# The merge stage of a one-core decoder layer: two passes over the column tiles, branch products from high and low parts, and the first weight tiles fetched during the attention

## The reference, cut to what matters

```
h = rms_norm(x, ln_mix_pre); z = h @ w_in
o_nsa = attend(...)                       # 512 features
o_gm  = u * chunk_spatial_mix(v, ...)     # 512 features
g_a, g_b = split(sigmoid(merge columns of z), 2)     # 2 x 1024 features
mixed = (g_a * (o_nsa @ w_branch_nsa) + g_b * (o_gm @ w_branch_gm)) @ w_out
x = x + rms_norm(mixed, ln_mix_post)
```

## Time and profile before

| what | us |
|---|---|
| runs of the kernel before: median (lowest to highest, 3 runs) | 2273.68 (2272.06 to 2279.49) |
| the profiled execution: its own time | 2271.01 |
| the profiled execution: span from first to last instruction | 2269.2 |
| merge stage: first matmul to last branch matmul's end | 884.61 to 1179.1 |
| merge stage, one tile in steady state | 18.29 |
| mean granted TensorE clock over the span | 0.953 |

### The profile page before, as it was taken

One profiled execution on the slowest core, in us unless ns is written; L12 is line 12 of the kernel. 1 busy time (PEld: TensorE's weight loads), 2 busy tenths in 40 slices (PEclk: granted clock), 3 DMA queues, 4 the chain that ended last, 5 costly groups with the idle time before them and its releaser, 6 DMA issues. The chain is left out here.

```text
span 2269.2 us, 33313 instructions
## 1 busy us (share of the span) xinstructions
PE 2082.9 (92%) x13581; PEld 1937.6 (85%) x13581; DVE 746.0 (33%) x1439; ACT 503.9 (22%) x917; POOL 571.6 (25%) x471
## 2 busy tenths in 40 slices
PE   6999999985688887999999799999999999997897
PEld 5999989953566776888879799999999999997786
DVE  3202533333766764111132343202321321234412
ACT  4112011122466564101021231110000000011323
POOL 1222400000344443112213213333323333331120
PEclk6999999987799998999999799999999999998898
DMA  5323264124200001111113121111111111113011
GB/s 165 113 75 125 53 217 161 62 110 166 82 1 2 2 1 29 48 44 42 42 46 111 49 94 46 37 56 47 44 42 54 47 35 58 47 35 126 24 46 77
DMA packets 164786, 150.88 MB, mean 66 GB/s; under 512 B 24747, under 2 KB 157389, under 8 KB 161934
## 3 DMA queue, kind: packets, MB, share of 16 engines
q1 hardware_dynamic: 160846, 111.68, 16.2%
q0 software_dynamic: 2304, 33.56, 3.7%
q10 hardware_dynamic: 1536, 4.23, 0.5%
HBM read 132.54 MB, written 21.10 MB: 68 GB/s over the span
## 5 line engine op out<-in xcount | busy, mean ns | idle before, releaser
L583 POOL CAST WS<-W 128x1024 fp32r<-128x1024 f32 (+2 forms) x126 | 124.7, 990 | 1139.8 <-PE ffn_acc L575 539.9
L575 PE MATMUL ffn_acc<-HH,WS 128*128 128x344 f32 x2112 | 394.8, 321 | 9.0 <-DVE HL L507 7.9
L575 PEld LDWEIGHTS ffn_acc<-HH,WS 128*128 128x128 f32 x2112 | 344.3, 189 | 9.4 <-issue 8.0
L585 POOL TENSOR_TENSOR WS<-W,WS 128x1024 fp32r<-128x1024 f32 (+2 forms) x126 | 297.2, 2358 | 10.1
L575 PE MATMUL ffn_acc<-HL,WS 128*128 128x344 f32 x1056 | 224.8, 321 | 0.0
L575 PE MATMUL ffn_acc<-AH,WS 128*128 128x344 f32 x1056 | 195.4, 320 | 0.0
L575 PE MATMUL proj_acc<-HH,WS 128*128 128x344 f32 x912 | 174.2, 323 | 6.2 <-DVE HL L507 6.2
L575 PEld LDWEIGHTS ffn_acc<-HL,WS 128*128 128x128 f32 x1056 | 179.4, 190 | 0.0
L575 PEld LDWEIGHTS ffn_acc<-AH,WS 128*128 128x128 f32 x1056 | 171.6, 188 | 0.0
L1844 POOL TENSOR_SCALAR Hr<-Hr,tiny,gtok 128x63 f32<-128x63 f32 (+4 forms) x192 | 124.4, 657 | 174.5 <-DVE tiny L1924 141.7
L575 PE MATMUL merge_acc<-HH,WS 128*128 128x344 f32 x768 | 149.6, 327 | 11.8 <-POOL WS L585 11.8
(11 more groups left out here) (374 smaller groups left out, 3163.6 us busy)
## 6 DMA issues: line engine op xcount, KB each, us to landing
W<-in_w_in SPq DMA_DIRECT2D x31, 512.0 KB, 4.1
W<-in_w_ffn_gate SPq DMA_DIRECT2D x22, 512.0 KB, 3.8
W<-in_w_ffn_up SPq DMA_DIRECT2D x22, 512.0 KB, 3.9
X<-kept_x SPq DMA_DIRECT2D x2, 4128.0 KB, 13.3
W<-in_w_ffn_down SPq DMA_DIRECT2D x16, 384.0 KB, 3.4
W<-in_w_ffn_down SPq DMA_DIRECT2D x16, 320.0 KB, 3.1
kept_x<-Z SPq DMA_DIRECT2D x1, 4128.0 KB, 15.6
Z<-kept_x SPq DMA_DIRECT2D x1, 4128.0 KB, 13.8
```

What stands on the lines that cost most here:

```text
L575: last = k.nc.tensor.matmul(acc[:, s, n, 0:NW], k.WS[:, ws, part, c, :], src[:, c, n * NW:(n + 1) * NW], start=(c == 0 and part == 0 and s ...
L583: k.nc.gpsimd.tensor_copy(k.WS[:, ws, 0, 0:nk, :], w).then_inc(hi_done, 1)
L585: k.nc.gpsimd.tensor_tensor(k.WS[:, ws, 1, 0:nk, :], w, k.WS[:, ws, 0, 0:nk, :].bitcast(F32), ALU.subtract).then_inc(split_done, 1)
```

## The change

The 16 tiles are no longer a loop; they are written out in the order j = 1 for m = 0 to 7, then j = 0 for m = 0 to 7. The first pass writes its gated product straight into `MT`, the second puts its own into `TM` and adds it to `MT`.

The branch product is made like the gate product. At the head of each pass ScalarE rounds the four chunks of the branch activation into `BH` (`high`), and VectorE subtracts them in place to get the low parts `OGL` or `ONL` (`lows`). GpSimd splits each branch weight tile into one buffer `WB`. TensorE issues the three products per chunk: 36 matmuls in place of 12. There is one `BH` for both passes: ScalarE makes the second pass's high parts behind the branch product of tile 7 (the eighth), and VectorE makes its low parts behind the scaling of tile 8 (the ninth).

SyncE fetches the gate weights and the branch weights of the first tile at the beginning of the attention into columns of the `kvtok` area that the attention leaves free. GpSimd splits the gate tile from there in two halves.

```diff
         k.WS = place("WS", "CW", [P, 2, 2, DC, P], F32R)
-        k.E = sb("E", [P, 5632])
+        k.E = place("E", "E", [P, 5632])
+        k.WB = place("WB", "E", [P, 2, 4, P], F32R, 4 * N)
+        k.BH = place("BH", "Z", [P, 4, N], F32R, 8 * N)
+        k.OGL = place("OGL", "Z", [P, 4, N], F32R, 13104)
+        k.ONL = place("ONL", "Z", [P, 4, N], F32R, 17232)
...
             sp.dma_start(k.X[:].rearrange("p c t -> p (c t)"), k.kept).then_inc(x_back, 16)
+            sp.dma_start(k.kvtok[:, 0:8, 256:384], weight(k.g["w_in"], GB0)).then_inc(k.first_in, 16)
+            sp.dma_start(k.kvtok[:, 0:4, 512:640], weight(k.g["w_branch_gm"], 0)).then_inc(k.first_in, 16)
+            sp.wait_ge(k.first_in, 32)
...
+        tiles = [(j, m) for j in (1, 0) for m in range(8)]
...
         @block.sync
         def _(sp):
+            for u, (j, m) in enumerate(tiles):
+                if u == 0:
+                    continue
+                if u > 1:
+                    sp.wait_ge(split_done, u)
+                sp.dma_start(k.W[:, 0, 0:8, :], weight(w, m * P + (GA0, GB0)[j])).then_inc(k.wfull[0], 16)
+                if u > 1:
+                    sp.wait_ge(bw_done, u)
...
         @block.tensor
         def _(pe):
+            for u, (j, m) in enumerate(tiles):
+                if u == 0:
+                    pe.wait_ge(split_half, 1)
+                    split_tile(k, acc, 0, 0, k.HH, k.HL, 4, more=True, wait=(pe, h.lo_done))
+                    pe.wait_ge(split_done, 1)
+                    split_tile(k, acc, 0, 0, k.HH, k.HL, DC, first=4, wait=(pe, h.lo_done)).then_inc(gates_done, 1)
+                else:
+                    pe.wait_ge(split_done, u + 1)
+
+                    pe.wait_ge(scaled, u)
+                    split_tile(k, acc, 0, u % 2, k.HH, k.HL, DC).then_inc(gates_done, 1)
+                pe.wait_ge(bw_done, u + 1)
+                if u:
+                    pe.wait_ge(gated, u)
+                for c in range(4):
+                    if m == 0:
+                        pe.wait_ge(b_lo, 4 * (1 - j) + c + 1)
+                    for part, src in ((0, k.BH), (0, low[j]), (1, k.BH)):
+                        for n in range(NT):
+                            last = nc.tensor.matmul(acc[:, 1, n, 0:NW], k.WB[:, part, c, :], src[:, c, n * NW:(n + 1) * NW],
...
         @block.gpsimd
         def _(pool):
+            pool.wait_ge(k.first_in, 32)
+            for b in range(2):
+                c = slice(4 * b, 4 * b + 4)
+                nc.gpsimd.tensor_copy(k.WS[:, 0, 0, c, :], first_gate[:, c, :]).then_inc(hi_done, 1)
...
+            for u, (j, m) in enumerate(tiles):
+                if u:
+                    pool.wait_ge(k.wfull[0], base[0] + 16 * u)
+                    if u >= 2:
+                        pool.wait_ge(gates_done, u - 1)
+                    split_weights(k, pool, 0, u % 2, DC, hi_done, u + 1, split_done)
...
+                    pool.wait_ge(k.wfull[1], base[1] + branch[0])
+                    pool.wait_ge(branch_done, u)
+                wb = k.W[:, 1, 0:4, :] if u else first_branch
+                nc.gpsimd.tensor_copy(k.WB[:, 0], wb).then_inc(bw_hi, 1)
+                pool.wait_ge(bw_hi, u + 1)
+                nc.gpsimd.tensor_tensor(k.WB[:, 1], wb, k.WB[:, 0].bitcast(F32), ALU.subtract).then_inc(bw_done, 1)
...
         @block.scalar
         def _(act):
...
+            high(1)
+            for u, (j, m) in enumerate(tiles):
+                if u == 8:
+                    act.wait_ge(branch_done, 8)
+                    high(0)
...
         @block.vector
         def _(dve):
...
+                nc.vector.tensor_tensor(tokens(SA[:, u % 2, :]), acc[:, 0, :, 0:NW], tokens(k.R1[:]), ALU.mult).then_inc(scaled, 1)
+                if u == 8:
+                    lows(0)
+                dve.wait_ge(sig, u + 1)
+                dve.wait_ge(branch_done, u + 1)
+                if j == 1:
+                    nc.vector.tensor_tensor(tokens(k.MT[:, m, :]), tokens(SA[:, u % 2, :]), acc[:, 1, :, 0:NW], ALU.mult).then_inc(gated, 1)
```

More of the change, by code:

```diff
@@ L104, in build @@
         base = -(-nc.sbuf_base // 32) * 32
-        sizes = {"X": DC * N, "H": DC * N, "Z": 21360, "W": 2048, "CW": 4096}
+        sizes = {"X": DC * N, "H": DC * N, "Z": 21360, "W": 2048, "CW": 4096, "E": 5632}
         sb("slab", [P, sum(sizes.values()) + 8])
@@ L126, in build @@
         k.WS = place("WS", "CW", [P, 2, 2, DC, P], F32R)
-        k.E = sb("E", [P, 5632])
+        k.E = place("E", "E", [P, 5632])
[3 more added lines that the diff above has]
+        k.ONL = place("ONL", "Z", [P, 4, N], F32R, 17232)
+        k.first_in = ctx.enter_context(nc.semaphore("first_in"))
         k.R1 = sb("R1", [P, N])
@@ L1959, in merge @@
         acc = st.psum("acc", [P, 2, NT, 512])
-        mm = st.sems("gates_done branch_done")
-        scaled, sig, gated, merged, slot_open, hi_done, split_done, slot_ok = st.sems(
-            "scaled sig gated merged slot_open hi_done split_done slot_ok")
+        gates_done, branch_done, scaled, sig, gated, merged, hi_done, split_half, split_done, bw_hi, bw_done, b_hi, b_lo = st.sems(
+            "gates_done branch_done scaled sig gated merged hi_done split_half split_done bw_hi bw_done b_hi b_lo")
         SA = chunks(k.E[:, 0:2 * N], 2)
@@ L1966, in merge @@
         base = list(k.wcount)
-        k.wcount[0] += 8 * 32 + 16
-        k.wcount[1] += 8 * 48
+        k.wcount[0] += 16 * 16
+        k.wcount[1] += 7 * 16 + 8 * 32
         nsa = g["w_branch_nsa"].rearrange("(gr c d) m -> gr d c m", gr=2, d=HD)
+        raw = (k.ON, k.OG)
+        low = (k.ONL, k.OGL)
+        tiles = [(j, m) for j in (1, 0) for m in range(8)]
+        first_gate, first_branch = k.kvtok[:, 0:8, 256:384], k.kvtok[:, 0:4, 512:640]
         block = st.block()
@@ L1973, in _ @@
         def _(sp):
[L1974 to L1987, removed]
+            for u, (j, m) in enumerate(tiles):
[6 more added lines that the diff above has]
+                    sp.wait_ge(bw_done, u)
+                if j == 0:
+                    for gr in range(2):
+                        sp.dma_start(k.W[gr * HD:(gr + 1) * HD, 1, 0:4, :], nsa[gr][:, :, m * P:(m + 1) * P]).then_inc(k.wfull[1], 16)
+                else:
+                    sp.dma_start(k.W[:, 1, 0:4, :], weight(g["w_branch_gm"], m * P)).then_inc(k.wfull[1], 16)
+            sp.wait_ge(split_done, 16)
             sp.dma_start(k.W[:, 0, 0:8, :], weight(g["w_out"], 0)).then_inc(k.wfull[0], 16)
@@ L1991, in _ @@
         def _(pe):
[L1992 to L2003, removed]
+            for u, (j, m) in enumerate(tiles):
[4 more added lines that the diff above has]
+                    split_tile(k, acc, 0, 0, k.HH, k.HL, DC, first=4, wait=(pe, h.lo_done)).then_inc(gates_done, 1)
+                else:
+                    pe.wait_ge(split_done, u + 1)
[10 more added lines that the diff above has]
+                            last = nc.tensor.matmul(acc[:, 1, n, 0:NW], k.WB[:, part, c, :], src[:, c, n * NW:(n + 1) * NW],
+                                                    start=(c == 0 and part == 0 and src is k.BH), stop=(c == 3 and part == 1))
+                last.then_inc(branch_done, 1)
@@ L2005, in _ @@
         @block.gpsimd
         def _(pool):
[L2007 to L2017, removed]
@@ L2018, in _ @@
-            split_weights(k, pool, 0, 0, DC, hi_done, 16, split_done)
+            pool.wait_ge(k.first_in, 32)
+            for b in range(2):
+                c = slice(4 * b, 4 * b + 4)
+                nc.gpsimd.tensor_copy(k.WS[:, 0, 0, c, :], first_gate[:, c, :]).then_inc(hi_done, 1)
+                pool.wait_ge(hi_done, b + 1)
+                nc.gpsimd.tensor_tensor(k.WS[:, 0, 1, c, :], first_gate[:, c, :], k.WS[:, 0, 0, c, :].bitcast(F32),
+                                        ALU.subtract).then_inc(split_half if b == 0 else split_done, 1)
@@ new lines, in _ @@
+            branch = [0]
+            for u, (j, m) in enumerate(tiles):
[4 more added lines that the diff above has]
+                    split_weights(k, pool, 0, u % 2, DC, hi_done, u + 1, split_done)
+                    branch[0] += 32 if j == 0 else 16
+                    pool.wait_ge(k.wfull[1], base[1] + branch[0])
[4 more added lines that the diff above has]
+                nc.gpsimd.tensor_tensor(k.WB[:, 1], wb, k.WB[:, 0].bitcast(F32), ALU.subtract).then_inc(bw_done, 1)
@@ L2020, in _, with high @@
+            pool.wait_ge(k.wfull[0], base[0] + 16 * 16)
+            pool.wait_ge(gates_done, 15)
+            split_weights(k, pool, 0, 0, DC, hi_done, 17, split_done)
         @block.scalar
         def _(act):
+            def high(j):
+                for c in range(4):
+                    nc.scalar.activation(k.BH[:, c, :], raw[j][:, c, :], ACT.Copy).then_inc(b_hi, 1)
             for c in range(DC):
                 h.scalar(act, c)
[L2024 to L2027, removed]
+            high(1)
@@ L2029, in _, with lows @@
+            for u, (j, m) in enumerate(tiles):
+                if u == 8:
```

(26 more changed lines are left out.)

## The result

The changed kernel takes 2250.28 us, the median of 4 runs (2246.35 to 2257.94), beside 2272.87 for 4 runs of the kernel before on the same chip (2268.66 to 2279.49). The ratio is 0.9916, with an interval from 0.9895 to 0.9936: 22.6 us, or 0.8%, faster. The forecast was 2252, with a range of 2245 to 2261. The profiled execution took 2254.18 us, with a span of 2252.4.

The account below looks back on a forecast made before the run. The prediction took TensorE, busy 92%, to bound the kernel. Tiles 18.6 + head 6.4 - tile 8's wait 2.7 - clock 1.0 = 21.3 us gained, giving 2252 us, with 8 in 10 between 2245 and 2261.

Parts of the forecast that it names:

- The tiles: Merge tiles: cheaper branch product takes each from 18.29 to 17.05 us, gaining 18.6 us over 15 tiles.
- Hidden work at 0: Merge tiles and attention: added GpSimd splits, VectorE work and early transfers stay hidden behind TensorE or other waits, costing 0.
- The head: Start of the merge: weights already there, so tile 0's branch product ends at 898.1 instead of 904.5, gaining 6.4 us.
- Tile 8's wait: Change of passes: TensorE waits 2.7 us for VectorE's first low part before tile 8's branch product.
- Its clock: Behind tile 8's wait: TensorE's clock may fall to 0.50; 1.0 us charged, between none and 2.0.
- The sum: Whole kernel: 18.6 + 6.4 - 2.7 - 1.0 = 21.3 us gained, forecast 2252 us.
- The rivals: Two alternatives: early fetch gives no front gain (2259 us, chance 0.20), or GpSimd sets the pace (2304 us, 0.03).
- The fetch does not pay: Merge head: early weights only move TensorE's wait into the tile; front gain 0, sum 14.9, 2259 us; chance 0.20.
- GpSimd sets the pace: Merge tiles: late branch splits make TensorE wait, 15 tiles losing 51.6 us, net 30 us slower, 2304; chance 0.03.
- What would show it: Merge signs: tiles of 17.05 us, first matmul near 877, tile 0's branch ending near 898, one 2.7 us wait.
- the signs of being wrong: Merge: tile 0's HL ending after 894, clock under 1.00 elsewhere than behind tile 8's wait, per-tile waits, tiles above 17.2 us.

Follow-up runs that it names:

- float32 experiment: Changed kernel with the branch product again in float32 from unsplit operands; merge stage 302.71 us, beside 308.28 in the kernel before and 287.86 in the changed one.
- held-back split: Changed kernel with GpSimd holding back tile 1's gate split until the eight HL are done; merge stage 284.14 us, 3.7 less.
- early lows: Changed kernel with the second pass's four lows ahead of VectorE's wait for tile 8's gate product; 2250.9 us beside 2277.3, merge stage 283.62 us.

## Why the prediction was right

**The tiles, 18.6 us: right.** Gate 11.35, branch 5.67, tile 17.03 to 17.07 us, where 11.37, 5.68 and 17.05 were worked out. The pace of the output projection carried over exactly. The float32 experiment shows that the gain is the product's.

**Hidden work at 0: right.** TensorE waits for GpSimd nowhere in the merge, and still would not with five times the branch split. The fetch costs the attention nothing that can be seen: from its first load to the merge's first `HH` it takes 299.63 us before and 299.91 after. These are the first loads, of the kernel before and of the changed one:

```profile
574.65 0.33 SPq L1690 DMA_DIRECT2D X<-kept_x  x1
...
578.53 0.33 SPq L1695 DMA_DIRECT2D X<-kept_x  x1
```

**The head, 6.4 us: right in kind, 5.8 measured.** The `HL` were forecast at 15.5 us and took 16.02. Two readings behind the 15.5 were off, and they nearly cancelled. An `HL` alone lasts 1.29 us, but the next one starts 1.205 us behind it; the first four in the kernel before, with next to nothing of GpSimd beside them:

```profile
875.47 4.91 DVE L507 SCALAR_TENSOR_TENSOR HL<-X,gains,HH 128x1032 fp32r<-128x1032 f32 x4 [5.10 <-ACT HH L502]
```

So eight alone take 4.91 + 4 x 1.205 = 9.73 us, not 10.3, and GpSimd's work costs more than the 0.66 us per us that was used: (16.02 - 9.73) / 7.85 = 0.80 here and, by the same count, 0.83 in the merge before and 0.74 in the project stage. TensorE started 3.21 us behind the first `HH`; 3.0 was forecast. The Trainium skill (SBUF — State Buffer, "Who interferes with whom") would have charged the full 7.85. For VectorE this trace shows 6.3, which is four fifths of that and not two thirds.

Where VectorE was running first, GpSimd waited. In the earlier trace rows its cast began while the fourth `HL` ran, and took 2.13 us where it takes 1.04 elsewhere. In the held-back split it took 5.34, a little longer than the four `lows` that had begun 0.22 us before it, and these took the same 4.65 as without it. Why it waited for one instruction there and for four here is not shown.

**Tile 8's wait, 2.7 us: right** (2.55), with VectorE's lows as the releaser, as named.

**Its clock, 1.0 us: too small here.** Tile 8 lost 4.23 us, of which the wait is 2.55; the other 1.7 is the stretch of 3.41 us at 0.50. The charge was halfway between two rows that disagreed, and both cases came: the clock fell behind the wait in three of the four profiles where tile 8 is as in the change, and not in the held-back split. The Trainium skill (TensorE: Matmul & The Clock Gate, "HAM oscillation") describes a return to half rate behind each of a loop's waits, which were longer than this one; these runs show it in three of four at 2.55 us. What decides it stays open.

**The sum.** 18.6 + 5.8 - 4.2 = 20.2 us, and the stage shows 20.4, where 21.3 was forecast. The medians moved by 22.6 and 23.7. The difference of 2 to 3 us lies within the interval of the ratios (14 to 24 us in the first session), and other stages vary by more than that from run to run. The two profiled executions, for example, differ by only 16.8 us: in the changed one the merge began 4.2 us later (878.44 for 874.28), and 3.9 of these were there already at the attention's first load. I do not attribute the difference; that the median came within 2 us of the forecast is in part luck.

The times named under "What would show it" are those of the run before. Less the 4.2 us, the first matmul stands at 877.5 and the last `HL` ends at 891.5, where 877.3 and 891.0 were forecast; none of the signs of being wrong came.

**The rivals.** "The fetch does not pay" fell: without it the stage is 3.8 us longer. Its mechanism is real in part, as VectorE gives back some 1.9 us of the 5.6 us of earlier start. "GpSimd sets the pace" fell, with the margin shown.

## What to carry to other kernels

When work comes off an engine that is busy without a gap, the gain is the pace of a stage that already runs the new form, and here it came out to a few hundredths; the uncertainty lay at the seams, where a pipeline starts or changes its input. At a seam, look for work whose inputs are ready long before its place in the list: the four lows cost 4.2 us behind a wait that they didn't need and nothing ahead of it. At a head, moving a load earlier pays only until the next engine is late, so move the work behind the load too, into the gap of an earlier stage.

## What the runs showed of the hardware

A wait of 2.55 us dropped TensorE's clock in one run and one of 2.56 us left it alone in another. The clock varies far more from run to run in a stage that the change does not touch. These are 50 us around the head of the feed-forward stage, in the kernel before, the changed one and the one with early lows (the clock is the third number from the end):

```profile
1270.00:1320.00 50.00, 37.77 (x223) 36.92 (x221) 30.94 (x29) 17.27 (x17) 6.70 (x4) 0.73 0.15 43
```

```profile
1254.00:1304.00 50.00, 37.90 (x248) 36.99 (x246) 31.31 (x29) 19.66 (x19) 6.70 (x4) 0.80 0.15 43
```

```profile
1248.00:1298.00 50.00, 38.95 (x192) 38.10 (x191) 28.91 (x28) 15.56 (x16) 7.79 (x4) 0.62 0.15 43
```

About the same part of the program has 0.73, 0.80 and 0.62, which is about 27, 20 and 38 us at 0.50. That is one source of several us between whole runs. With early lows, what stands behind the merge took 4.1 us longer than in the changed kernel's profiled execution (1090.2 and 1086.1 us), about as much as the merge had gained; the longer stretch at 0.50 fits that, but no run isolates it.

Three matmuls on split parts, 3 x 0.158 = 0.47 us, are cheaper than the one float32 matmul of the same 128x344 that they replace, 0.57 us.
